# Weight tiles of 4 chunks by 512 columns for the last down projection and the attention values, token block by token block

## The reference, cut to what matters

```
k, v = shared_kv(x, ...)          # h = rms_norm(x, kv_norm)
v = (h @ w_v).reshape(B, S, 8, 128)     # h: 256 x 1024, w_v: 1024 x 1024
```

```
y = hidden @ w_down_2             # 256 x 2816 times 2816 x 1024
out = x + rms_norm_2(y, g)        # mean square over the 1024 columns of a token
```

## Time and profile before

| what | value |
| --- | --- |
| median of three executions | 1215.7 us (1215.48 to 1219.0) |
| span of the profiled execution, core 0 | 1218.9 us (its own time is not listed apart; the nearest of the three is 1219.0, 0.1 more) |
| TensorE busy, of the span | 97% |
| VectorE (DVE), ScalarE (ACT) busy | 72%, 50% |
| TensorE share of the chain that ended last | 83% |
| mean granted TensorE clock | 0.984 |
| DMA, mean of the span | 163 GB/s |

### The profile page before, as it was taken

The page is one execution under the profiler, slowest core; times in us unless marked ns, Lnnn a source line. Parts: engine busy times, 40 slices in busy tenths (PEclk is TensorE's granted clock), DMA queues, the critical chain, the costliest instruction groups (busy, mean ns, idle before and its releaser), DMA issues.

```text
span 1218.9 us, 24046 instructions
## 1 busy us (share of the span) xinstructions
PE 1176.6 (97%) x9142; PEld 1120.1 (92%) x9142; DVE 876.5 (72%) x1480; ACT 611.4 (50%) x1072; POOL 63.7 (5%) x53
## 2 busy tenths in 40 slices
PE   9999999999999999998999999999979899999997
PEld 9988898999999999778989999999967589999997
DVE  6999886676665587565767666566896757999954
ACT  6764654544445444344445444455455745656542
POOL 0576000000000000000000000000000000000000
PEclk9999999999999999999999999999988889999999
DMA  7554453455556556214525555555553213545563
GB/s 280 175 199 145 139 173 104 139 174 187 191 173 204 180 184 237 76 44 182 173 70 173 194 185 172 184 200 189 209 195 118 70 36 122 173 172 185 190 208 108
DMA packets 32008, 198.42 MB, mean 163 GB/s; under 512 B 3776, under 2 KB 6080, under 8 KB 9024
## 3 DMA queue, kind: packets, MB, share of 16 engines
q1 hardware_dynamic: 29440, 193.09, 45.9%
q10 hardware_dynamic: 2496, 4.33, 1.1%
HBM read 194.12 MB, written 1.05 MB: 160 GB/s over the span
## 4 chain that ended last, share of the span: by engine, by line
PE 83%; DVE 10%; ACT 3%; issue 2%; DMA 2%; ACTq 0%; DVEq 0%; SPq 0%
PE acc L490 21%; PE acc L492 21%; PE acc L491 21%; PE acc L526 7%; PE acc L506 2%; DVE wlo L1455 2%; PE acc L773 2%; DMA raw<-weights 2%; DVE wlo L1450 1%; PE sc L737 1%; PE tp L490 1%; PE tp L491 1%; PE tp L492 1%; PE st L641 1%; PE tp L762 1%
## 5 line engine op out<-in xcount | busy, mean ns | idle before, releaser
L490 PE MATMUL acc<-Hhi,whi 128*128 128x256 f32 x1368 | 389.4, 285 | 4.0 <-DVE wlo L1455 3.9
L491 PE MATMUL acc<-Hlo,whi 128*128 128x256 f32 x1368 | 387.1, 283 | 0.0
L492 PE MATMUL acc<-Hhi,wlo 128*128 128x256 f32 x1368 | 387.1, 283 | 0.0
L1003 ACT ACTIVATE whi<-raw 128x1024 fp32r<-128x1024 f32 x160 | 169.2, 1058 | 358.1 <-PE acc L492 329.0
L1450 DVE TENSOR_TENSOR wlo<-raw,whi 128x1024 fp32r<-128x1024 f32 (+1 forms) x158 | 193.4, 1224 | 116.8 <-ACT whi L1003 115.4
L490 PEld LDWEIGHTS acc<-Hhi,whi 128*128 128x128 f32 x1368 | 262.5, 192 | 5.3 <-DVE wlo L1455 3.4
L491 PEld LDWEIGHTS acc<-Hlo,whi 128*128 128x128 f32 x1368 | 262.6, 192 | 0.2
L492 PEld LDWEIGHTS acc<-Hhi,wlo 128*128 128x128 f32 x1368 | 262.5, 192 | 0.0
L1455 DVE TENSOR_TENSOR wlo<-raw,whi 128x1024 fp32r<-128x1024 f32 (+1 forms) x158 | 193.3, 1223 | 1.6 <-ACT whi L1006 0.4
L490 PE MATMUL acc<-FH,whi 128*128 128x256 f32 x608 | 173.0, 285 | 4.9 <-DVE FH L2085 3.3
L492 PE MATMUL acc<-FH,wlo 128*128 128x256 f32 x608 | 171.6, 282 | 0.0
(11 more groups left out here) (356 smaller groups left out, 2024.6 us busy)
## 6 DMA issues: line engine op xcount, KB each, us to landing
raw<-weights SPq DMA_DIRECT2D x177, 1024.0 KB, 4.9
MEM<-mem_in SPq DMA_DIRECT2D x2, 1024.0 KB, 7.5
held<-weights SPq DMA_DIRECT2D x2, 1024.0 KB, 6.0
E<-A ACTq DMA_DIRECT2D x12, 128.0 KB, 2.2
X<-x_in ACTq DMA_DIRECT2D x4, 256.0 KB, 5.3
raw<-weights SPq DMA_DIRECT2D x4, 256.0 KB, 6.4
MEM<-consts ACTq DMA_DIRECT2D x2, 512.0 KB, 4.8
out<-MKV SPq DMA_DIRECT2D x4, 256.0 KB, 2.1
```

The source lines that it names most:

```text
L490: pe.matmul(dst, w, x, start=first, stop=False)
L491: pe.matmul(dst, w, xl, start=False, stop=False)
L492: return pe.matmul(dst, wl, x, start=False, stop=last)
L1003: act.activation(whi[j][:, 0:HALF, 0:width], raw[j][:, 0:HALF, 0:width], ACT.Copy).then_inc(hi_out, 1)
```

## The change

Both stages get tiles of another form: 4 chunks of 128 rows by 512 weight columns, again 1 MB. In the host code `broad` makes them for `w_v_shared` and `w_down_2`. On TensorE `broad_tile` goes over the token blocks, and in each over the chunks of the tile, with 512 streamed columns a matmul and a whole bank as the target.

- `diffv` (`shared_values`): two column groups of two tiles. The first group fills the banks `acc[0]` and `acc[1]`, one for each token block, the second two banks of `sc`. TensorE waits once, ahead of the first tile, for both `acc` banks. DVE reads out with two instructions of 128x512 behind tiles 1 and 3.
- `down2` (`broad_down`): two column groups of 6 tiles (five of 4 chunks, one of 2 chunks), each group in two banks of `sc`. In the second group tiles 4 and 5 are taken together: first both of them for token block 0, then both for token block 1, each with its own `tile_done`.
- Behind it, squares, gain, sum, inverse root and the output come for each token block apart, in instructions of 128x512; token block 0 has its turn while TensorE works on block 1.

```diff
@@ in the list of TensorE @@
-            down("down2", "up2", turned=True)
+            broad_down()
-                stage("diffv", Hhi, Hlo, turned=True)
+                shared_values()
+            def broad_tile(j, banks, xhi, xlo, chunks, k0, end, tts=range(NT)):
+                for tt in tts:
+                    o = slice(tt * P, (tt + 1) * P)
+                    for k, c in enumerate(chunks):
+                        w, wl = (t[j][:, 2 * (k + k0):2 * (k + k0) + 2, :] for t in (whi, wlo))
+                        mm = three(banks[tt], xhi[:, c, o], xlo[:, c, o], w, wl, c == 0, c == end - 1)
+                return mm
+            def shared_values():
+                for o in range(2):
+                    for part in range(2):
+                        t = 2 * o + part
+                        tile_in(L0["diffv"] + t)
+                        if t == 0:
+                            pe.wait_ge(acc_free, G0["diffv"] + 2)
+                        banks = [acc[tt][:, :, :] for tt in range(NT)] if o == 0 else [halves(sc[:, tt, :]) for tt in range(NT)]
+                        broad_tile(part, banks, Hhi, Hlo, range(HALF * part, HALF * part + HALF), 0, DC).then_inc(tile_done, 1)
+            def broad_down():
+                for o in range(2):
+                    banks = [halves(sc[:, 2 * o + tt, :]) for tt in range(NT)]
+                    for q in range(6):
+                        tile_in(L0["down2"] + 6 * o + q)
+                        chunks = range(HALF * q, min(HALF * q + HALF, FC))
+                        if o == 0:
+                            pe.wait_ge(s_h, h.at("up2", chunks[-1] // 2 + 1))
+                        if o == 1 and q >= 4:
+                            continue
+                        broad_tile(q % 2, banks, FH, FL, chunks, 0, FC).then_inc(tile_done, 1)
+                for tt in range(NT):
+                    for q in (4, 5):
+                        chunks = range(HALF * q, min(HALF * q + HALF, FC))
+                        mm = broad_tile(q % 2, banks, FH, FL, chunks, 0, FC, (tt,))
+                    mm.then_inc(tile_done, 1)
@@ in the list of ACT @@
+            def last_down():
+                for t in range(10):
+                    ahead("down2", t // 6, 6, t % 6)
+                    if t == 5:
+                        act.wait_ge(s_sq, sq.at("post"))
+                        for tt in range(NT):
+                            last_squares(0, tt)
+                for tt in range(NT):
+                    act.wait_ge(tile_done, T0["down2"] + 11 + tt)
+                    last_squares(1, tt)
...
@@ in the list of DVE @@
+            def last_down():
+                for t in range(10):
+                    ahead("down2", t // 6, 6, t % 6)
+                    if t == 5:
+                        dve.wait_ge(rows_loaded, 2 * 16)
+                        for tt in range(NT):
+                            dve.wait_ge(s_sq, sq.at("down2", tt + 1))
+                            gained(0, tt)
+                for tt in range(NT):
+                    dve.wait_ge(s_sq, sq.at("down2", 3 + tt))
+                    gained(1, tt)
+                    final, summed = rt[:, RT["fpost2"], tt:tt + 1], total[:, tt:tt + 1]
+                    link(dve.reduce_sum(summed, sums_of[:, SUMS["fpost2"], tt:tt + 1, 0:2], axis=AX_X))
+                    link(inverse_root("fpost2", 1, D, RMS_EPS, final, sums=summed))
+                    for half in range(2):
...
```

More of the change, by code:

```diff
@@ L618, in group @@
                                     o = slice(m * P, (m + 1) * P)
[L619 to L624, removed]
                                     mm = three(acc[g][:, m, :], whi[j][:, k - 8 * part, o], wlo[j][:, k - 8 * part, o],
@@ L1046, in square_sums, with last_squares @@
                 ins.then_inc(s_sq, 1)
+            def last_squares(o, tt):
+                act.activation(halves(SQ[:, 4 * o + 2 * tt:4 * o + 2 * tt + 2, :].rearrange("p a b -> p (a b)")), halves(sc[:, 2 * o + tt, :]),
+                               ACT.Square, accum_out=sums_of[:, SUMS["fpost2"], tt, o:o + 1]).then_inc(s_sq, 1)
             def last_down():
[L1050 to L1065, removed]
+                for t in range(10):
[7 more added lines that the diff above has]
+                    last_squares(1, tt)
             def residual(name, per, outs):
@@ L1556, in norm_columns, with gained @@
                 inverse_root(name, n, div, eps, rt[:, RT[name], 0:n]).then_inc(rt_ready, 1)
+            def gained(o, tt):
+                return dve.tensor_tensor(out=M2[:, 4 * tt + 2 * o:4 * tt + 2 * o + 2, :], in0=halves(sc[:, 2 * o + tt, :]),
+                                         in1=gain_rows["g_fpost2"][:, 2 * o:2 * o + 2, :], op=ALU.mult)
             def last_down():
[L1560 to L1575, removed]
-                    dve.wait_ge(s_sq, sq.at("down2", t + 1))
-                    dve.sem_inc(acc_free, 1)
-                    if t == 1:
-                        ahead("down2", i, 6, ks[-1])
@@ L2036, in to_tokens, with shared_values @@
                 link(dve.tensor_copy(rt[:, RT[name], 0:NT], st[:, 0:NT]))
[L2038 to L2051 removed]
+            def shared_values():
+                to_tokens("attn1")
+                ahead("diffv", 0, 4, 0)
+                for o in range(2):
+                    tile("diffv", 0, 4, 2 * o + 1)
+                    for tt in range(NT):
+                        src = acc[tt][:, :, :] if o == 0 else halves(sc[:, tt, :])
+                        ins = dve.tensor_scalar(MKV[:, 2 * DC + 4 * o + tt:2 * DC + 4 * o + tt + 3:2, :], src,
+                                                rt[:, RT["attn1"], tt:tt + 1], None, op0=ALU.mult)
+                        out_acc(ins)
+                    ahead("diffv", 0, 4, 2 * o + 1)
+                    if o == 0:
+                        ahead("diffv", 0, 4, 2)
             for layer in range(2):
@@ L2287, in plain, with broad @@
             tiles.append(column_tile(m, in_heads(order, c)))
+    def broad(m):
+        for c in range(0, D, 2 * MB):
+            for k in range(0, m.shape[0], HALF * P):
+                part = m[k:k + HALF * P, c:c + 2 * MB]
+                tile = np.zeros((HALF * P, 2 * MB), m.dtype)
+                tile[:part.shape[0]] = part
+                tiles.append(tile.reshape(HALF, P, 2 * MB).transpose(1, 0, 2).reshape(P, KC * MB))
     def halves(m, width):
```

34 lines of the change are left out of this document (8 added, 26 removed).

## The result

In six runs each the changed kernel took 1224.1 us at the median (1220.5 to 1227.2) and the kernel before 1217.4 us (1215.5 to 1220.5). The ratio is 1.0048, with a 95% interval of 1.0032 to 1.0064, so the change costs 5.8 us (3.9 to 7.8). The forecast was +2.7 us and "the same"; its slow side, for which it named 1222.3 us, came nearer. 1224.1 us lies above the range, which ended at 1223.0.

The account below looks back on a forecast made before the run. TensorE bounds the kernel by its matmul pace and waits. `down2` -3.2 + 0.3 + 1.2 + 3.85 + 1.7, tail -0.7, `diffv` -1.3 + 0.3 + 0.5 make +2.7 us: 1218.4 us, range 1213.7 to 1223.0.

Parts of the forecast that it names:

- the pace in `down2`: `down2` matmuls: 512 columns take 0.2244 us, a fixed rest paid once for each matmul; 3.2 us less.
- the clock term: Last 36 matmuls of `down2`: 3.4 us at half speed after the 3.85 us wait, 1.7 us lost, bounds 0 to 2.4.
- the tail: After the last matmul: 4.95 us of serial work for token block 1, 0.7 us less, bounds 0 to 1.0.
- signs named for being wrong: `down2`: last wait under 3 us, pace outside 0.214 to 0.237, or a wait for DMA among the matmuls.
- The last wait: `down2`, ahead of tile 10: TensorE stands while tile 11 is split into tile 9's buffer; 3.85 us, bounds 3.5 to 5.
- rival 2: Both stages: rest paid by the column, no gain in pace, waits remain; +6.6 us, 1222.3 us; chance 0.20.
- The pace in `diffv`: `diffv` matmuls: 512 columns take 0.2267 us by the same fixed rest; 1.3 us less.
- rival 1: Both stages: long streams hide the rest of the pace, 0.216 us a matmul; -0.3 us, 1215.4 us; chance 0.25.
- The wait of tile 1: `down2`: tile 1 is ready at 1153.86 but wanted at 1153.73; 0.3 us at most.
- the short tile: `down2`: tile 5's 12 matmuls, 2.69 us, don't cover the 3.85 us until tile 6 is ready; 1.2 us of wait.
- `diffv`'s waits: `diffv`: 0.3 us at the start for both `acc` banks, 0.5 us at the end for DVE's longer read-out.
- The base: Whole kernel: the sum of +2.7 us was put on the median of 1215.7 us, giving 1218.4 us.

Follow-up runs that it names:

- e7: Changed kernel with `down2` loading `Hhi` and `Hlo` instead of `FH` and `FL`; one execution, 0.2267 us a matmul, no ratio given.
- e4: Changed kernel with 30 extra unused f32 matmuls of 128 columns behind tile 9 of `down2`; ratio to the kernel before 1.0042.
- e3: Changed kernel with the wait for tile 11 moved behind token block 0's 12 matmuls on tile 10; ratio to the kernel before 1.0007.
- e5: Changed kernel with tiles 10 and 11 each passing both token blocks in turn, block 0 not finished first; ratio to the kernel before 1.0003.
- e8: Changed kernel with first group cut 4, 4, 4, 4, 3, 3, tile 11's wait moved and only its used half split; ratio to the kernel before 0.9972.
- e10: Changed kernel run again without an edit; ratio to the kernel before 1.0043.
- e2: Kernel before with only the new `down2`, `diffv` left as it was; ratio to the kernel before 1.0050.
- e6: Changed kernel with each 512-column matmul of `down2` issued as two of 256 columns; ratio to the kernel before 1.0047.
- e9: Changed kernel with 15 extra unused f32 matmuls of 128 columns behind tile 9 of `down2`; ratio to the kernel before 1.0025.

## Why the prediction was wrong

The step that failed is the pace in `down2`, taken as a fixed rest for each matmul; beside it the clock term was too small. The waits and the tail came as forecast. 2.7 us were forecast, 5.8 (3.9 to 7.8) measured, and 1224.1 us is 1.1 above the range's end. None of the signs named for being wrong came: the last wait (3.69) and the pace (0.2311) stayed within their bounds, and no wait for a DMA stands among the matmuls. In the order of the terms:

- **The pace in `down2`, forecast -3.2 us: failed.** It was taken as a fixed cost of 11.1 ns a matmul, which 512 columns would pay once. Measured are 17.8 ns beside the 213.3 of the columns, so -1.3 us: 1.9 us of the error, of which 0.2 are a slip (528 x 0.1178 = 62.2 less 59.2 is 3.0; the 62.4 was counted to the stream's end). If the pace is a part for the matmul and a part for its columns, the two widths from the same buffers give 0.1178 = a + b and 0.2311 = a + 2b: of the 11.1 ns some 4.5 go with the matmul and 6.6 with its 256 columns. That split fits two points and is no more than that: with the other operand, in `diffv`, 0.1205 and 0.2267 leave nothing for the columns. Forecast and rival 2 were each half right. The reason given, that at the low clock 256 columns take 0.21 us and nothing beside it, told nothing of what is paid for by the column at the high clock, as the prediction itself had said.
- **The pace in `diffv`, forecast -1.3: right**, 0.2267 us. The same rule applied to another loaded operand held there, and e7 shows that the operand makes the difference; why is not shown, and the prediction had no reason to expect the rule to hold for one operand and not for the other, so the hit is in part luck. The 0.216 of rival 1 occurred nowhere; the earlier trace rows were also misread, since an unsplit f32 call leaves two records (e4), so eight records are four calls, of 0.43 us each. The Trainium skill ("TensorE: Matmul & The Clock Gate", section "Back-to-back issue gap") would have 215.8 ns for 512 columns by its formula, which it gives for a single matmul by itself; no stage of this trace has it, 226.7 and 231.1 were measured.
- **The last wait, forecast +3.85: right**, 3.86, and by the mechanism named (e3, e5).
- **The clock behind it, forecast +1.7: too small.** It was 1.7 in the first profile, but 2.4 as a mean of five and up to 2.9, beyond the bound of 2.4. The forecast took one fall, of 3.4 us, from the earlier trace rows as if its length were a constant. 0.7 us of the error. The trace of the kernel before already had a fall twice as long, behind the 4.28 us of the earlier trace rows, the wait nearest in length to the forecast's 3.85:

```profile
910.00:912.00 2.00, 0.00 (x0) 0.00 (x0) 1.93 (x5) 1.92 (x3) 0.00 (x0) 0.86 0.00 0
...
918.00:920.00 2.00, 2.00 (x17) 1.29 (x15) 0.27 (x1) 1.17 (x2) 0.00 (x0) 0.93 0.99 414
```

  With 0.50 in the three windows between, that is 0.56 + 6.0 + 0.28 = 6.8 us, and it began ahead of TensorE's start at 913.70. The prediction had only read the durations of the first matmuls there, and these don't tell: 0.38 stands in the earlier trace rows behind the 1.40 us after which the clock held.
- **The wait of tile 1, +0.3, and of the short tile, +1.2:** 0.1 and 1.0. Right; e8, which removes the short tile, shows its wait gone, while the one at tile 1 stands there as before.
- **The tail, -0.7:** 0.9. That block 0 would be "just in time" held: 0.21 us of idle time before block 1's product.
- **`diffv`'s waits, +0.3 and +0.5:** 0.25 and 0.53. Right, and the clock held behind the 1.50.
- **The base:** the sum was put on a median of three runs, 1215.7 us; six runs gave 1217.4. 1.7 of the 5.7 us between forecast time and measured time are that, and without them the time would lie inside the range; that it lies outside is owed to the base as much as to the terms. The ratio isn't touched by it. Nor is it by the 0.1 us that the prediction took to lie around the span: in all profiled executions since, 1.8 us do.

Summed again with what was measured: `down2` -1.3 + 0.1 + 1.0 + 3.86 + 2.4 = +6.1, tail -0.9, `diffv` -0.4: +4.8 us, inside the measured 3.9 to 7.8. The middle of the interval is 1 us higher, that of e10 (1.0043) 0.4; whether that is real stays open.

The chances carried the same fault. Rival 2 was to decide "from about 0.227 us a matmul on", and the pace was 0.2311; and the measured 0.48% is above the 0.3% from which it would say slower. With the pace between the forecast's value and the rival's, and a clock term that can only be longer than the shortest fall seen, "slower" should have had the larger half, not 0.34.

## What to carry to other kernels

A wait placed ahead of work that doesn't need it costs the whole latency of what it waits for, and on TensorE the slow clock behind it on top: here 3.86 and 2.4 us, to save 2.4 us of tail, and moving one wait behind 12 matmuls left 0.8 us of idle time and kept the tail. Where two buffers take turns, count for each tile what the engine has to do in the other one against the time to refill (3.85 us here), and above all at short tiles and where the order of the loops turns. And an overhead seen at one size is two unknowns, a part for the instruction and a part for its length: keep both ends in the sum when the size doubles. A fallen clock is not priced from one fall either: 3.4 and 6.8 us at half speed stand in the same trace here.

## What the runs showed of the hardware

- The pace of these split matmuls depends on the buffer of the loaded operand: 0.2267 us for 512 columns with `Hhi` and `Hlo`, 0.2311 with `FH` and `FL`, the same instructions and streamed tiles otherwise (e7, one execution).
- The same idle time of 3.69 us was followed by 3.4 us at a granted clock of 0.50 in one execution and by 6.8 in four others (changed; e2, e6, e7, e10). In those four the clock had fallen before TensorE resumed; in the first it fell 0.9 us behind that. Behind 0.83 and 0.34 us it stayed at 1.00 (e3, e9), and matmuls whose results nobody uses held it through the same wait (e9).
- The length of one idle time alone doesn't decide: in the kernel before the clock fell at 942.2 as well (0.54 in the window 942 to 944), where TensorE had been idle for no longer than 0.47 us at a time in the six us before.
- An unsplit f32 matmul of 128 columns is two records in the trace and takes 0.22 to 0.23 us a call (e4: 30 calls in 6.6 us, e9: 15 in 3.51).
